# Block two with half of its weight slots' low parts precomputed, its indexer block first, and filler transposes ahead of norms

## The reference

```python
h = rms_norm_2(x, attn_norm_g[l])
proj = h @ w_in[l]                                   # 1024 x 3656
(mq, mk, mv, dq, dk, dv, sq, sk, sv, iq, ik, iw) = jnp.split(proj, offsets, axis=-1)
moba = moba_attention(qk(mq), qk(mk), split_heads(mv))          # 4 heads, causal
diff = diff_attention(dq1, dq2, dk1, dk2, split_heads(dv), lam) # 4 heads, two score maps
diff = rms_norm_2(diff, diff_subln_g[l]) * (1.0 - lam_init)
# indexer: score = sum_h w[h] * relu(iq[h] . ik), top 64 causal keys per query
dsa = dsa_attention(qk(sq), qk(sk), split_heads(sv), iq_h, ik_r, iw * (IDX_HEADS ** -0.5))
x = x + jnp.concatenate([moba, diff, dsa], -1) @ w_out[l]
x = x + (silu(h2 @ w_gate[l]) * (h2 @ w_up[l])) @ w_down[l]     # h2 = rms_norm_2(x), width 2816
```

## Time and profile before

| | |
|---|---|
| median of 3 runs (lowest to highest) | 1750.43 us (1750.07 to 1750.53) |
| the profiled execution's own time | 1748.0 us |
| its span in the profile | 1745.9 us |
| TensorE matmul busy | 1614.8 us, 92% |
| VectorE busy | 1049.1 us, 60% |
| ScalarE busy | 731.8 us, 42% |
| GpSimd busy | 99.2 us, 6% |
| mean granted TensorE clock | 0.965 |
| DMA | 257.69 MB, mean 148 GB/s |

### The profile page before, as it was taken

One profiled execution on the slowest core, in us unless ns is written; L12 is line 12 of the kernel. 1 busy time (PEld: TensorE's weight loads), 2 busy tenths in 40 slices (PEclk: granted clock), 3 DMA queues, 4 the chain that ended last, 5 costly groups with the idle time before them and its releaser, 6 DMA issues.

```text
span 1745.9 us, 22902 instructions
## 1 busy us (share of the span) xinstructions
PE 1614.8 (92%) x9050; PEld 1309.9 (75%) x9050; DVE 1049.1 (60%) x1599; ACT 731.8 (42%) x1246; POOL 99.2 (6%) x88
## 2 busy tenths in 40 slices
PE   6999889999999989989999897789999887789999
PEld 3865676788888866569988675579998666579997
DVE  3537654533443356666644867758874767768873
ACT  3425523421342224635533544444443444444542
POOL 1010000000000001000000301000000201000000
PEclk9999999999999989999999989899999999899999
DMA  9348224432333324848666632246656432246653
GB/s 358 111 154 312 101 89 135 131 96 89 94 97 95 97 72 133 290 131 268 182 191 184 173 108 83 67 122 183 187 185 189 134 109 83 72 124 186 185 183 119
DMA packets 174218, 257.69 MB, mean 148 GB/s; under 512 B 10448, under 2 KB 92640, under 8 KB 173984
## 3 DMA queue, kind: packets, MB, share of 16 engines
q1 hardware_dynamic: 171872, 250.38, 45.9%
q0 software_dynamic: 2016, 5.77, 1.3%
q10 hardware_dynamic: 224, 0.07, 0.0%
HBM read 255.15 MB, written 1.05 MB: 147 GB/s over the span
## 4 chain that ended last, share of the span: by engine, by line
PE 81%; DVE 11%; issue 3%; ACT 2%; DMA 1%; POOL 1%; SPq 0%; POOLq 0%; DVEq 0%; ACTq 0%
PE bank L1764 49%; PE pair_bank L1764 20%; DVE w_lo L1270 2%; PE bank L1816 2%; PE bank L2015 1%; PE pair_bank L1987 1%; PE pair_bank L2033 1%; PE bank L1998 1%; DVE wide L1354 1%; PE bank L1928 1%; DVE rope_a L1420 1%; POOL xrstd L848 1%; DVE head_sq L1428 1%; DMA raw<-in_w_ada 1%; DVE proj L1448 1%
## 5 line engine op out<-in xcount | busy, mean ns | idle before, releaser
L1270 DVE TENSOR_TENSOR w_lo<-raw,w_hi 128x1024 fp32r<-128x1024 f32 x374 | 450.1, 1219 | 304.8 <-ACT w_hi L962 301.9
L962 ACT CAST w_hi<-raw 128x1024 fp32r<-128x1024 f32 x374 | 386.7, 1044 | 391.1 <-PE bank L1764 315.2
L1764 PE MATMUL pair_bank<-act_hi,w_hi 128*128 128x256 f32 (+1 forms) x736 | 230.4, 313 | 9.9 <-DVE act_lo L1344 4.5
L1764 PE MATMUL pair_bank<-act_hi,w_lo 128*128 128x256 f32 (+1 forms) x736 | 227.0, 308 | 0.0
L1764 PE MATMUL pair_bank<-act_lo,w_hi 128*128 128x256 f32 (+1 forms) x736 | 226.8, 308 | 0.0
L1764 PE MATMUL bank<-w_hi,act_hi 128*128 128x512 f32 (+2 forms) x528 | 218.2, 413 | 4.2 <-DVE w_lo L1270 2.2
L1764 PE MATMUL bank<-w_hi,hid_lo 128*128 128x512 f32 x560 | 221.4, 395 | 0.0
L1764 PE MATMUL bank<-w_hi,hid_hi 128*128 128x512 f32 x560 | 221.3, 395 | 0.0
L1764 PE MATMUL bank<-w_lo,hid_hi 128*128 128x512 f32 x560 | 221.3, 395 | 0.0
L1764 PE MATMUL bank<-w_lo,act_hi 128*128 128x512 f32 (+2 forms) x528 | 209.8, 397 | 0.0
L1764 PE MATMUL bank<-w_hi,act_lo 128*128 128x512 f32 (+2 forms) x528 | 208.9, 396 | 0.0
(11 more groups left out here) (227 smaller groups left out, 2103.9 us busy)
## 6 DMA issues: line engine op xcount, KB each, us to landing
raw<-in_w_mlp SPq DMA_DIRECT2D x128, 512.0 KB, 3.7
raw<-in_w_ada SPq DMA_DIRECT2D x96, 512.0 KB, 5.7
raw<-in_w_in SPq DMA_DIRECT2D x72, 512.0 KB, 3.6
raw<-in_w_gate SPq DMA_DIRECT2D x44, 512.0 KB, 3.7
raw<-in_w_up SPq DMA_DIRECT2D x44, 512.0 KB, 3.7
raw<-in_w_down SPq DMA_DIRECT2D x44, 512.0 KB, 3.5
raw<-in_w_out SPq DMA_DIRECT2D x32, 512.0 KB, 3.8
raw<-in_w_in SPq DMA_DIRECT2D x16, 256.0 KB, 3.0
```

The source lines that it names most:

```text
L962: nc.scalar.copy(hi_of(i)[:, 0:w], raw[:, i % RAW, 0:w]).then_inc(hi_ready, 1)
L1270: nc.vector.tensor_tensor(w_lo[:, i % RAW, 0:w], raw[:, i % RAW, 0:w], hi_of(i)[:, 0:w].bitcast(F32), ALU.subtract).then_inc(lo_ready, 1)
L1764: ins = nc.tensor.matmul(o, a[x], b[y], start=first and i == 0, stop=True, skip_group_check=True)
```

## The change

Five edits go together.

1. The column blocks of `rows2` are ordered anew, and two are cut differently. Before: dq, dk, iq, dv, ik (with iw, 72 columns, one slot of 8 row tiles), mqk, sqk, mv with sv (512 columns). After: iq, mv with ik and iw (328 columns, slots of 3, 3 and 2 row tiles), dq, dk, dv, mqk, sqk, sv (256 columns, two slots of 4 row tiles). `FILL2` and `OUT2` are written anew for it.
2. 32 "early" slots (16 of each layer's 29 in `rows2`) are put into the first MLP of block one, one behind each weight slot from the 11th on. SyncE loads them, ScalarE and VectorE make their parts, TensorE does nothing with them, and GpSimd's queue stores the low part in DRAM.
3. When such a slot comes up in `rows2` it is "known": SyncE loads `raw` as before, ScalarE casts, VectorE does nothing, and SyncE loads `w_lo` from DRAM three slots later (`known_low`).
4. `keep_busy`: 28 transposes of the unit matrix into bank 7, put on TensorE ahead of its waits for normed rows, in `norm2` (four times), in `rows1` of layer one and at the head of `up1` (twice).
5. Output projection of block two: other banks for its four accumulators, and its wait for bank 2 stands only ahead of the one that uses it.

The diff, cut to its core:

```diff
-SPLIT2, MIXES = 6, 6
+SPLIT2, MIXES, BUSY = 6, 6, 28
+EARLY_SLOTS = (1, 3, 5, 8, 10, 12, 14, 15, 17, 18, 20, 21, 23, 24, 26, 28)
+EARLY_AT, EARLY_EVERY, BEHIND = 10, 1, 3
+EARLY = [(l, s) for l in range(DEPTH) for s in EARLY_SLOTS]
...
-        BLOCKS2 = (("dq", DQ), ("dk", DK), ("iq", IQ), ("dv", DV), ("ik", IK), ("mqk", MQ), ("sqk", SQ), ("mv_sv", MV))
+        BLOCKS2 = (("iq", IQ), ("mv_ik", IK), ("dq", DQ), ("dk", DK), ("dv", DV), ("mqk", MQ), ("sqk", SQ), ("sv", SV))
...
+            4: [("first", 0), ("second", 0)],
+            5: [("first", 1), ("second", 1), ("turn", 0)],
+            6: [("drain", 1, 0), ("drain", 1, 1), ("turn", 1)],
+            7: [("first", 2), ("second", 2), ("index_scale",), ("turn", 2), ("logits", 0)],
+            8: [("logits", 1)],
...
+            16: [("second", 5), ("first", 6), ("turn", 5)],
+            17: [("second", 6), ("turn", 6), ("score", 0)],
+            18: [("drain", 4, 0), ("weigh", 0), ("drain", 4, 1), ("search", 0, 2), ("score", 1)],
+            19: [("weigh", 1), ("mix", 0), ("search", 0, 2), ("score", 2)],
...
+            23: [("weigh", 5), ("mix", 4), ("first", 7), ("score", 6)],
+            24: [("weigh", 6), ("mix", 5), ("second", 7), ("square", 0), ("first", 8), ("turn", 7), ("score", 7)],
+            25: [("weigh", 7), ("mix", 6), ("second", 8), ("turn", 8), ("norm", 0), ("score", 8)],
+            26: [("drain", 6, 0), ("weigh", 8), ("mix", 7), ("drain", 6, 1), ("search", 1, 1), ("score", 9)],
+            27: [("weigh", 9), ("mix", 8), ("first", 9), ("square", 1), ("score", 10)],
+            28: [("drain", 7, 0), ("weigh", 10), ("mix", 9), ("drain", 7, 1), ("second", 9), ("first", 10), ("norm", 1), ("turn", 9), ("score", 11)],
...
+            0: [("weigh", 11), ("mix", 10), ("second", 10), ("turn_rows", 0), ("turn", 10), ("turn_rows", 1), ("score", 12)],
+            1: [("weigh", 12), ("mix", 11), ("search", 1, 2), ("score", 13)],
+            2: [("weigh", 13), ("search", 1, 3), ("mix", 12), ("score", 14)],
+            3: [("weigh", 14), ("mix", 13), ("score", 15)],
+            4: [("weigh", 15), ("mix", 14)],
...
+        for x in range(len(EARLY)):
+            FILL["mlp1", 0].setdefault(EARLY_AT + x * EARLY_EVERY, []).append(("early", x))
...
+        def freed(e, i):
+
+            if n.slots[i][0] == "early":
+                e.wait_ge(lo_stored[i % RAW], 16 * n.at(f"lo_stored{i % RAW}", i))
+            else:
+                e.wait_ge(multiplied, n.at("multiplied", i))
...
+            def known_low(self, i):
+
+                if i < 0 or n.slots[i][0] != "known":
+                    return
+                x, r, u = n.value["known", i], i % RAW, n.slots[i][1]
+                was = n.value["early", x]
+                self.e.wait_ge(lo_stored[was % RAW], 16 * n.at(f"lo_stored{was % RAW}", was))
+                self.e.wait_ge(hi_ready, n.at("hi_ready", i))
+                self.e.dma_start(w_lo[:, r, 0:u].bitcast(F32), split_lo[x, :, 0:u]).then_inc(lo_loaded[r], 16)
+                n.put(f"lo_loaded{r}", i)
...
+            def early(self, x):
+                i = n.value.get(("early", x), 0)
+                u = n.slots[i][1]
+                self.e.wait_ge(lo_ready, n.at("lo_ready", i))
+                self.e.dma_start(split_lo[x, :, 0:u], w_lo[:, i % RAW, 0:u].bitcast(F32)).then_inc(lo_stored[i % RAW], 16)
+                n.put(f"lo_stored{i % RAW}", i)
...
-                    self.e.wait_ge(multiplied, n.at("multiplied", hi_before(i)))
+                    before = hi_before(i)
+                    if n.slots[before][0] == "early":
+                        self.e.wait_ge(lo_ready, n.at("lo_ready", before))
+                    else:
+                        self.e.wait_ge(multiplied, n.at("multiplied", before))
...
-                if i >= len(n.slots) or n.slots[i][0] == "ada":
+                if i >= len(n.slots) or n.slots[i][0] in ("ada", "known"):
...
+            def keep_busy(self):
+
+                if 7 in self.ada_before:
+                    self.e.wait_ge(mod_ready, n.at("mod_ready", self.ada_before[7]))
+                for i in range(BUSY):
+                    nc.tensor.transpose(bank[7][:, i % 4 * P:(i % 4 + 1) * P], ident, ident)
```

More of the change, by code:

```diff
@@ L322, in build @@
             3: [("drain", 0, 0), ("drain", 0, 1)],
[L323 to L343, removed]
@@ new lines, in build @@
+            7: [("first", 2), ("second", 2), ("index_scale",), ("turn", 2), ("logits", 0)],
+            8: [("logits", 1)],
+            9: [("logits", 2)],
+            10: [("drain", 2, 0), ("drain", 2, 1), ("logits", 3)],
+            11: [("first", 3), ("logits", 4)],
+            12: [("second", 3), ("first", 4), ("turn", 3)],
+            13: [("second", 4), ("turn", 4), ("logits", 5)],
+            14: [("drain", 3, 0), ("drain", 3, 1), ("search", 0, 3)],
+            15: [("first", 5), ("search", 0, 1)],
@@ L572, in extras @@
                         self.norm_half(*args)
+                    elif what == "early":
+                        self.early(*args)
                     elif what == "split":
@@ L618, in split, with early @@
             def split(self, i): pass
+            def early(self, x): pass
             def unit(self, l, r): pass
@@ L708, in put, with put2 @@
                 n.slots.append((kind, used))
+                self.known_low(self.i - BEHIND)
                 self.i += 1
+            def known_low(self, i):
[7 more added lines that the diff above has]
+                n.put(f"lo_loaded{r}", i)
+            def put2(self, kind, l, s):
+                nk, wd, parts = rows2_pieces(l, s)
+                self.put(kind, nk * wd, lambda r: [(tiles(r[:, 0:nk * wd], nk)[:, :, cs], x) for cs, x in parts])
+            def early(self, x):
+                n.value["early", x] = self.i
+                self.put2("early", *EARLY[x])
             def start(self):
@@ L935, in ahead, with early @@
                 self.split(self.i + k)
+            def early(self, x):
+                self.step()
             def attend(self, l):
@@ L1859, in norm2 @@
                 e = self.e
+                self.keep_busy()
                 for t in range(TT):
@@ L2057, in mix @@
                     for t in range(TT):
-                        e.wait_ge(drained, n.at("drained", ("rows2", l, BLOCK2["dv" if st["diff"] else "mv_sv"], t)))
+                        e.wait_ge(drained, n.at("drained", ("rows2", l, BLOCK2["dv" if st["diff"] else "mv_ik" if st["group"] == 2 else "sv"], t)))
                     if st["group"] in (1, 2):
@@ L2170, in rows2 @@
                 step = 0
-                for j, name, c, ns, nk, wd in rows2_blocks():
-                    for q in range(ns):
+                for j, name, c, wd, slots in rows2_blocks():
+                    k0 = 0
+                    for q, nk in enumerate(slots):
                         w = self.take(nk)
@@ L2183, in rows2 @@
                                 ins = self.three(b[:, 0:wd], self.act_of(k, 2 + t), [v[:, kk, :] for v in w], k == 0)
-                            if q == ns - 1 and t == 0:
+                            if q == len(slots) - 1 and t == 0:
                                 self.filled(ins, ("rows2", l, j, t))
-                        self.took(ins, ("rows2", l, j, 1) if q == ns - 1 else None)
+                        self.took(ins, ("rows2", l, j, 1) if q == len(slots) - 1 else None)
                         self.extras2(FILL2, l, step)
                         step += 1
+                        k0 += nk
             turn_before = None
```

105 lines of the change are left out of this document (60 added, 45 removed).

## The result

Device time, median: 1737.16 us after (1735.23 to 1738.31, 4 runs) against 1750.48 before (1750.07 to 1751.96, 4 runs); ratio 0.992, 95% interval [0.9905, 0.9936]. The change is 13.3 us faster. The forecast was 1720, 30 us faster; less than half of that gain came.

What follows compares the result with a forecast made beforehand. The prediction took TensorE, 81% of the chain, as the bound. Its terms 7+5+6+11+1+0 = 30 us, off the profiled 1748.0, gave 1718.0, and with 2.4 us for timed runs 1720 us; range 1704 to 1742.

Steps and rivals of the forecast that it cites:

- steps 1 and 2: Block two's projections: new block order streams faster, 7 us; the clock fall in the 72-wide block goes, 5 us.
- other lower-clock time: Lower-clock time mostly around the waits of the stage's tail, which keeps as many: 1 us gained (-3 to +8).
- step 4: Block two's stage: low parts from DRAM spare VectorE 16 splits per layer, so TensorE idles less: 11 us gained.
- step 3: Seven waits for normed rows: added unit transposes hold the clock for the work behind: 6 us gained (0 to 10).
- step 5: First feed-forward: the 32 early slots' loads, casts, splits and stores are hidden: 0 us (-8 to 0).
- Rival D: First feed-forward: early slots aren't hidden, through ScalarE's delayed drain of the hidden tile: 1728 us, chance 0.05.
- idle list: Block two's stage: TensorE's waits after the change, listed per layer, sum to 20.0 us against 25.5 and 25.9.
- the bank-2 chain: Block two's stage: two diff turns around unit 10 share bank 2, costing TensorE 2.3 us idle per layer.
- step 1: Block two's projections: blocks 328 and 256 wide replace 72 and 512, streaming 7 us less (0 to +10).
- A: Block two's stage: waits only move, the tail eats what the splits free, fourth term 0: 1731 us, chance 0.14.
- C: Block two's sixteen attention steps: chains outlast their one slot of cover, stalling 2.0 us each; slower, 1758 us, chance 0.09.

Runs made afterwards that it cites:

- e3: The changed kernel with early slots kept away from the middle of the first down projection (the seam), four more at the feed-forward's end: 1729.52 us.
- e12: e3 with one order-list exchange: at step 24 of the order lists the differential rows' squares come behind unit 8's first half: 1722.93 us.
- e2: The changed kernel with no early slots, VectorE splitting all 29 slots of each block two again: 1740.04 us.
- e9: The changed kernel's block order and order lists alone, without early slots or unit transposes: 1747.20 us.
- e7: e3 with 32 more unit transposes in the wait ahead of weighing 11 and 22 ahead of score 14, in both layers: 1718.66 us.
- e13: e7 with 26 unit transposes ahead of weighing 7, in the 3.3 us wait: 1714.42 us.
- e5: e3 without the unit transposes ahead of the seven norms: 1737.14 us.
- e4: The kernel before the change with only the unit transposes ahead of the seven norms added: 1748.82 us.
- e8: e3 with 14 real matmuls of the identity with itself ahead of each norm instead of the 28 transposes: 1729.81 us.

## Why the prediction was wrong

The gain can be split in two ways. The first compares the two profiled executions: TensorE's busy time in the stages fell by 11.0 us, where the block order and the clock (steps 1 and 2 and "other lower-clock time") had 13. Its idle time there fell by 4.7, where step 4 had 11. The five other stretches became 2.0 shorter, where step 3 had 6. The feed-forward became 6.0 longer, where step 5 had 0. The second is a ladder of medians from before to after: the order alone -3.2 us (1750.4 to 1747.2), the transposes on it -7.2 (to 1740.0), the low parts with early slots off the seam -10.5 (to 1729.5), the seam +7.6 (to 1737.2). The two agree on the seam. They differ on the rest, because on the ladder the order's rung has falls of the clock that the later rungs take away again. Each rung's size holds for this sequence only.

- **Step 5 (0 us) is the step that failed outright: 7.6 us lost by e3, 6.0 on the profile.** Steps 1 to 4 together gave 20.9 us (1750.4 to 1729.5), where the forecast had 30; step 5 took more than a third of that back. "ScalarE's cast of an early slot waits for the end of the current real slot" named the right resource, but followed it to one engine only, to ScalarE's own drain. The follower that counts is on VectorE: the early slot's split, and behind it the residual update for which TensorE's banks wait at the change of column halves. Rival D's place and mechanism are refuted too: away from the seam the 32 slots cost nothing that the runs can tell.
- **Step 4 (11 us): its idle list came out at 23.3 and 23.4 us, not 20.0.** That is 4.7 us gained on the profile, the largest shortfall there among steps 1 to 4. The list was right for steps 18 to 22 (forecast 1.0; 1.06 in layer one, step 23 with them), the bank-2 chain (2.3; 2.33), score 14 (2.9; 2.79), weighing 13 (2.5; 2.01) and 11 (4.8; 4.20). It missed the turns of units 3 to 6 (2.45 us, put down with 0.6 for "the rest") and was short behind them (4.4 for steps 23, 24 and 27; 6.55 at steps 24 to 28), mostly by VectorE's wait for the squares, as e12 shows. That the ladder gives 10.5 is no proof of the 11: of e3 against e2, 8.2 us are idle time and the rest clock, and part of it is waits and falls that the new order had brought.
- **Steps 1 and 2 with "other lower-clock time" (7+5+1 us): 11.0 on the profile, 3.2 as a rung.** The streaming came: 328 columns run 0.149 us apart (0.146 forecast), and the fall in the narrow block is gone. In e9 these two should have taken 6.9 us each (48x(0.340-0.268) twice, and (10.4+3.4)/2) off TensorE's busy time in the stages, and it fell by 3.9 and rose by 0.3, 3.6 together. Some 10 us went back, about half behind the turns in the middle of the stage and half in the tail. The sentence "the tail keeps as many, so I take 1 us (-3 to +8)" counted how much idle time the lists leave and not in how long pieces: in the kernel after the change the tails hold 7 us more at the lower level than before, 3.5 us lost for 1 gained. That the tail's waits are what makes the clock fall there is shown by e7 and e13, where the same waits filled with unit transposes hold it. For the falls in the middle no run isolates the cause; they went together with the longer waits of the turns.
- **Step 3 (6 us): 5.4 and 7.6 by removal, 7.2 on the ladder, 2.0 on the profile.** In the kernel changed it is right in size, but not shown to be right in its working: part of the gain lies in the stages (e5), and in the kernel before, e4 halved the lower-level time behind the norms and gained 1.6 us at most. The Trainium skill's rule ("TensorE: Matmul & The Clock Gate", Part 4: the transpose mode does not count as activity) is contradicted by e8. There 28 passes of real matmuls in place of 28 transposes give the same time and the same granted clock, 0.973, where e5 without either has 0.961.

In the prediction's step 1, "48 matmuls for each block and one of the three products" should read 48 for all three products of a block (8 row tiles, 2 token tiles, 3 products); its sum uses the right number.

Of the rivals, A's time (1731) was the nearest, but its reason holds only in part: the relief of VectorE gave 10.5 us (e3 against e2), and A's fourth term was 0. C didn't happen. Counted as C counts them, the sixteen steps hold TensorE 13.8 us in layer one, 0.9 each (13.3 and 0.8 forecast), where C decided from 1.8 on.

What stays open: why e4, the transposes in the kernel before, gave 1.6 us and not 6. The clock is higher in its runs, and their times go with the clock (1742.5 us at 0.974, 1754.1 at 0.965), and in the profiled one more of the stages passed at the lower level. Whether the transposes cause that or it is chance no run tells.

## What to carry to other kernels

Count a long wait of TensorE twice: once for its length, once for the work behind it at half the clock. Here each wait of 2.2 to 5.1 us in layer one's tail, in the kernel before, was followed by 3.4 or 6.8 us at the lower level, and the same idle time in waits far apart cost less than in two that lie close. Where such a wait can't be removed, unit transposes into a bank that is free there gave 10.9 and 4.2 us. They must fit in the wait, at the lower clock too: 26 in a wait of 1.3 us gained nothing, and 22 that met the lower clock ended 1.4 us late. And where work is added to an in-order engine's queue, look for what follows it at each change of phase, not in the steady state: one place in 64 steps cost 7.6 us, when the low parts gave 10.5.

## What the runs showed of the hardware

- After the change the clock fell to the lower level behind a wait of 3.87 us in otherwise dense streaming (0.50 from 411.4 to 414.8). In e7, with 0.61 us left of a wait of 4.20, the 23.5 us around it are at 1.00.
- Shorter waits went both ways: in e9 the clock fell behind a wait of 1.97 us (1427 to 1431), in the kernel before it stayed at 1.00 behind one of 2.04 (before 1448.32).
- A real 128x128 f32 matmul has two records of 0.12 us in the trace and took as long as two transposes. It held the clock neither better nor worse (e8).
- Lower-level time isn't lost time by itself: in e4 the lower-level time behind the norms halved, from 47.8 to 23.9 us, and the stretches with the norms changed by under 0.8 us each.
